# Last block's transposes and router products moved ahead of two panels and its second norm; deferred rows finished by VectorE in the second tile

## The reference

```python
shift1, scale1, gate1, shift2, scale2, gate2 = split(silu(cond) @ w_mod + b_mod, 6)
x = x + gate1 * rmsnorm(token_mixer(rmsnorm(x) * (1 + scale1) + shift1))
h = rmsnorm(x, g_pre2) * (1 + scale2) + shift2
x = x + gate2 * rmsnorm(hier_moe(h), g_post2)
# hier_moe: router products h @ w_rg (4 groups), h @ w_re (16 experts);
# best group, then the best 2 experts in it; for a chosen expert e:
#   a = silu(t @ w_eg[e]) * (t @ w_eu[e]);  y += gate[e] * (a @ w_ed[e])
```

## Time and profile before

| what | value |
|---|---|
| median of 3 runs | 684.89 us (684.49 to 685.68) |
| profiled execution, its own time | 689.32 us |
| its span | 687.6 us |
| PE busy | 656.3 us, 95% |
| DVE busy | 520.5 us, 76% |
| ACT busy | 416.5 us, 61% |
| POOL busy | 102.3 us, 15% |
| PE's share of the chain that ended last | 83% |
| mean rate of all transfers | 274 GB/s |

### The profile page before, as it was taken

One profiled execution on the slowest core, in us unless ns is written; L12 is line 12 of the kernel. 1 busy time (PEld: TensorE's weight loads), 2 busy tenths in 40 slices (PEclk: granted clock), 3 DMA queues, 4 the chain that ended last, 5 costly groups with the idle time before them and its releaser, 6 DMA issues.

```text
span 687.6 us, 10864 instructions
## 1 busy us (share of the span) xinstructions
PE 656.3 (95%) x3492; PEld 526.9 (77%) x3492; DVE 520.5 (76%) x756; ACT 416.5 (61%) x629; POOL 102.3 (15%) x150
## 2 busy tenths in 40 slices
PE   3999999999999999999989899999999999999983
PEld 0577767789999987778838688888888888888861
DVE  2667798656446468766579899999999999999966
ACT  5552222244434559884444578888888888888953
POOL 2030001055000000000013200000000000370361
PEclk9999999999999999999989999999999999999997
DMA  9975876539321243006798999999999999999586
GB/s 327 354 257 190 285 240 190 166 101 378 94 80 60 93 153 118 6 1 211 280 337 305 345 367 412 411 412 412 412 412 411 412 411 412 412 412 411 225 278 153
DMA packets 79002, 188.15 MB, mean 274 GB/s; under 512 B 7619, under 2 KB 29176, under 8 KB 78964
## 3 DMA queue, kind: packets, MB, share of 16 engines
q1 hardware_dynamic: 67456, 153.11, 60.3%
q0 software_dynamic: 7200, 22.47, 9.8%
q10 hardware_dynamic: 4310, 12.10, 4.4%
HBM read 166.12 MB, written 21.53 MB: 273 GB/s over the span
## 4 chain that ended last, share of the span: by engine, by line
PE 83%; DVE 6%; DMA 4%; SPq 2%; POOL 2%; issue 1%; ACT 1%; ACTq 0%; POOLq 0%; DVEq 0%
PE ps L2018 22%; PE ps L2038 11%; PE ps L1783 10%; PE ps L1843 8%; PE ps L1811 8%; PE ps L1815 5%; PE ps L1886 3%; PE ps L1716 3%; PE ps L1861 2%; PE ps L2001 2%; PE ps L1877 2%; SPq L403 2%; PE ps L1941 1%; DMA qkv_mem<-in_w_mod 1%; DMA catT_mem<-token_rows,token_lists 1%
## 5 line engine op out<-in xcount | busy, mean ns | idle before, releaser
L2018 PE MATMUL ps<-split_ring,split_rows 128*128 128x512 f32 x756 | 176.1, 392 | 1.2 <-DVE split_rows L1483 1.0
L2018 PEld LDWEIGHTS ps<-split_ring,split_rows 128*128 128x128 f32 x756 | 140.7, 188 | 30.5 <-DVE split_rows L1483 1.2
L1388 DVE TENSOR_TENSOR split_ring<-qkv_mem,split_ring 128x1024 fp32r<-128x1024 f32 x126 | 146.2, 1220 | 21.9 <-ACT split_ring L871 21.9
L871 ACT CAST split_ring<-qkv_mem 128x1024 fp32r<-128x1024 f32 x126 | 123.5, 1056 | 13.0 <-ACT catT_mem L995 9.2
L2038 PE MATMUL ps<-split_ring,split_rows 128*128 128x512 f32 x360 | 86.0, 394 | 0.0
L1811 PE MATMUL ps<-split_rows,split_ring 128*128 128x384 f32 x288 | 85.7, 345 | 0.2
L1815 PE MATMUL ps<-split_rows,split_ring 128*128 128x256 f32 x288 | 77.0, 280 | 0.0
L2038 PEld LDWEIGHTS ps<-split_ring,split_rows 128*128 128x128 f32 x360 | 66.5, 188 | 13.3
L1388 DVE TENSOR_TENSOR split_ring<-raw_ring,split_ring 128x1024 fp32r<-128x1024 f32 x64 | 74.2, 1221 | 0.0
L1783 PE MATMUL ps<-split_ring,split_rows 128*128 128x512 f32 x288 | 68.2, 393 | 0.0
L871 ACT CAST split_ring<-raw_ring 128x1024 fp32r<-128x1024 f32 x64 | 62.5, 1049 | 1.7 <-DMA raw_ring<-in_w_exp_up 1.7
(11 more groups left out here) (350 smaller groups left out, 928.0 us busy)
## 6 DMA issues: line engine op xcount, KB each, us to landing
qkv_mem<-in_w_exp_gate SPq DMA_DIRECT2D x64, 512.0 KB, 9.5
qkv_mem<-in_w_exp_up SPq DMA_DIRECT2D x60, 512.0 KB, 7.9
raw_ring<-in_w_exp_down SPq DMA_DIRECT2D x60, 512.0 KB, 9.5
raw_ring<-in_w_mod SPq DMA_DIRECT2D x28, 512.0 KB, 4.8
qkv_mem<-in_w_mod SPq DMA_DIRECT2D x32, 256.0 KB, 7.8
expert_rows<-catT_mem ACTq DMA_DIRECT2D x14, 512.0 KB, 6.7
expert_rows<-work POOLq DMA_DIRECT2D x26, 256.0 KB, 6.7
raw_ring<-in_w_in SPq DMA_DIRECT2D x12, 512.0 KB, 8.1
```

The costliest lines, as they stand in the source:

```text
L871: nc.scalar.copy(moe_split(tile, j, r, 0), moe_raw(tile, j, r)).then_inc(S["hi"], 1)
L1388: tt(moe_split(tile, j, r, 1), moe_raw(tile, j, r), moe_split(tile, j, r, 0).bitcast(F32), ALU.subtract).then_inc(S["lo"], 1)
L2018: ins = mm(ps[:, j, :], xS[:, s, k, :], moe_split(tile, j, k // 2, m)[:, (k % 2) * N:(k % 2 + 1) * N], start=(k == 0 and s + m == 0), stop ...
```

## The change

On PE, `row_transposes(4)`, `logits(3)` and `logits(4)` follow `late_panel(10, 0)` directly; `late_panel(11, 1)` comes after them. On DVE the last block's `second_norm` is cut in two: its reciprocal stays, its scale and shift move behind the ranking (`oh_ready`); the low part of the first gate panel's last quarter moves from there to behind `first_oh`. ACT issues the last block's rows for the gathers later (`h2_rows_out(4)`). POOL's four row operations leave POOL and become four DVE operations in the second tile, ahead of the early slots; POOL only issues the writes, behind its first two gathers. SP loads tile 1's gate panel before the first tile's up quarters, the up quarters 1 and 3 before 0 and 2, and `gate2` after all experts' weights.

```diff
 # SP
             late_half(10, 1)
+            expert_quarters((None, 1), 0, w_eg, slice(1, 2), (2, 3))
+            sp.wait_ge(S["mod_q"], MODQ + 6)
+            expert_quarters((None, 1), 0, w_eg, slice(1, 2), (0, 1))
+            sp.wait_ge(S["mod_q"], MODQ + 8)
+            expert_quarters((None, 0), 1, w_eu_first, slice(0, 1), (1, 3))
             sp.wait_ge(S["h2s"], TB)
             expert_quarters((None, 0), 1, w_eu_first, slice(0, 1), (0, 2))
-            sp.wait_ge(S["mod_q"], MODQ + 8)
-            expert_quarters((None, 0), 1, w_eu_first, slice(0, 1), (1, 3))
-            expert_quarters((None, 1), 0, w_eg, slice(1, 2))
             expert_quarters((None, 1), 1, w_eu, slice(1, 2))
-            sp.wait_ge(S["g_mm"], 2)
-            sp.wait_ge(S["modout0"], MODOUT + 16)
-            sp.wait_ge(S["modout1"], MODOUT + 16)
-            for c in range(2):
-                row_in(gate2, 5, c, S["gate_in"])
             expert_quarters((None, 1), 2, w_ed, slice(0, 1))
...
             expert_quarters((later, 2), 0, w_ed, expert_of((later, 1)))
+            sp.wait_ge(S["g_mm"], 2)
+            sp.wait_ge(S["modout0"], MODOUT + 16)
+            sp.wait_ge(S["modout1"], MODOUT + 16)
+            for c in range(2):
+                row_in(gate2, 5, c, S["gate_in"])
 # POOL
-            for n, c in enumerate(LATE):
-                pool.wait_ge(S["row_copied"], n + 1)
-                pool.wait_ge(S[f"modst{c % 2}"], MODST[c - 2] + 32)
-                pool.tensor_tensor(late_row(c), late_row(c), late_bias(c), ALU.add).then_inc(S["pool_chain"], 1)
-                pool.wait_ge(S["pool_chain"], n + 3)
-                pool.tensor_tensor(late_row(c), late_row(c), late_norm(c), ALU.mult).then_inc(S["mod_row"], 1)
-                pool.wait_ge(S["mod_row"], MOD_LATE - MOD_EARLY + n + 1)
-                pool.dma_start(mod_d[:, c * N:(c + 1) * N], late_row(c)).then_inc(S[f"modout{c % 2}"], 16)
...
+            for n, c in enumerate(LATE):
+                pool.wait_ge(S["mod_row"], MOD_LATE - MOD_EARLY + n + 1)
+                pool.dma_start(mod_d[:, c * N:(c + 1) * N], late_row(c)).then_inc(S[f"modout{c % 2}"], 16)
             with pool.Fori(0, last) as i:
 # ACT
             late_panel_out(1)
-            h2_rows_out(4)
...
             nc.scalar.activation(rw["e2"], rw["d2"], ACT.Exp).then_inc(S["exp0"], 1)
+            h2_rows_out(4)
 # DVE
             split_lo_moe((None, 0), 0, (2,))
-            second_norm(4)
-
+            dve.wait_ge(S["rt3s"], TB)
+            link(nc.vector.reciprocal(rs3[:, last_block:last_block + 1], rt3[:, last_block:last_block + 1]))
...
             tt(rw["d2"], rw["m2"], rw["m1"], ALU.subtract).then_inc(S["oh_ready"], 1)
 
-            split_lo_moe((None, 0), 0, (3,))
+            dve.wait_ge(S["norm2_in"], 64)
+            link(stt(h2[:, last_block, :], x[:, last_block, :], rs3[:, last_block:last_block + 1], scale2[:, 0, :], ALU.mult, ALU.mult))
+            tt(h2[:, last_block, :], h2[:, last_block, :], shift2[:, 0, :], ALU.add).then_inc(S["h2s"], 1)
             dve.wait_ge(S["cum_mm"], 1)
...
             ins.then_inc(S["first_oh"], 1)
+            split_lo_moe((None, 0), 0, (3,))
             dve.wait_ge(S["exp0"], len(UNITS) + 2)
...
             split_lo_moe((None, 1), 0, (3,))
+            for n, c in enumerate(LATE):
+                dve.wait_ge(S["row_copied"], n + 1)
+                dve.wait_ge(S[f"modst{c % 2}"], MODST[c - 2] + 32)
+                link(tt(late_row(c), late_row(c), late_bias(c), ALU.add))
+                tt(late_row(c), late_row(c), late_norm(c), ALU.mult).then_inc(S["mod_row"], 1)
 # PE
             late_panel(10, 0)
+            row_transposes(4)
             logits(3)
-            row_transposes(4)
+            logits(4)
+
             late_panel(11, 1)
-            logits(4)
-
             late_panel(10, 1)
```

More of the change, by code:

```diff
@@ L641, in _ @@
             pool.tensor_tensor(col(180), epsc, epsc, ALU.add).then_inc(S["pool_chain"], 1)
-            pool.wait_ge(S["pool_chain"], 3 + len(LATE))
+            pool.wait_ge(S["pool_chain"], 3)
             for b in range(TB):
```

## The result

The changed kernel takes 691.93 us (690.7 to 693.64, 4 runs) beside 685.28 (684.49 to 685.78, 4 runs) of the kernel before: ratio 1.0100, 95% interval 1.0074 to 1.0126. It is slower by 6.6 us where 2.05 us were forecast, and lies above the range. A second series gave 691.73 (690.62 to 698.0, 6 runs) beside 686.19: 1.0097 (1.0064 to 1.0130). Over 98 runs of the kernel before that went beside the experiments the median is 686.23, so the 684.89 on which the forecast stands was itself low by 1.3; against the wider base the loss is 5.5 to 5.7 us. Executions that took over 1.5% more than the fastest of their kernel are left out of every median here: one of the kernel before, two of e6 and one of e7.

What follows compares the result with a forecast made beforehand. PE, busy 95% of the span, was taken as the bound. Tile 1's gate product +0.1 us plus a PE stall of 1.95 gave +2.05: 684.89 to 686.9 us, 0.3% slower; range from 0.2 below 683.8 to 688.7.

Steps and rivals of the forecast that it cites:

- Part 1: PE's router products come earlier: logits(4) ends and DVE's ranking begins 1.98 us earlier.
- Part 2: DVE after the ranking: the moved norm, 2.46 us, spends the gain; L1450 starts about 0.1 us later.
- Part 3: POOL's row operations off DVE's list chain: four long steps shorten by 3.04 us together.
- Part 4: Later up quarters hold ACT, and with it DVE: quarter 0 lands at 363.3, `xT_lo` starts 1.35 us later.
- G: Start of tile 1's gate product on PE; forecast to move by +0.1 us (-1.2 to +1.4).
- Part 5: Four row operations on DVE, 2.7 us in all, stall PE once for 1.95 us within tile 1's 48 products.
- Part 6: Small parts: the later gather of tile 3, `gate2` at the end and later token rows each cost nothing.
- (a): Rival: up quarters in time, quarter 0 by 360.2, lists gain all 3.04; -1.1 us, 683.8; chance 0.17.
- (b): Rival: tile 1's gather lands sooner without `gate2` ahead, 2.9 us at most; -0.85 us, 684.0; chance 0.10.
- (c): Rival: PE's clock falls to half for a stretch after waits, 1.6 us more; +3.65 us, 688.5; chance 0.13.

Runs made afterwards that it cites:

- e6: Kernel before with the four row operations on DVE in the slack behind tile 1 and in tile 2, gate2 at the end: 685.34 us (0.9955 to 1.0009).
- e7: Changed kernel with 18 more idle-filling products on PE while it waits for the late rows' sums: 690.66 us (1.0041 to 1.0087).
- e8: Kernel before with PE's order alone changed: last transposes, both router products, then the two half panels: 686.81 us (0.9990 to 1.0025).
- e10: Kernel before with gate2 alone moved behind the last expert weights: 686.81 us (0.9989 to 1.0037).
- e11: Kernel before with SP's order alone changed: tile 1's gate panel ahead of the up panel, up quarters 1 and 3 before 0 and 2: 692.76 us.
- e17: Changed kernel with the norm back ahead of the ranking and SP's old order of the panels: 685.86 us (0.9976 to 1.0022).
- e3: Kernel before with the deferred rows moved to DVE at the changed kernel's place, gate2 at the end: 689.92 us (1.0022 to 1.0070).
- e9: e8 plus the row operations on DVE in the slack, POOL's writes behind its gathers, gate2 at the end: 684.07 us (0.9951 to 1.0000).
- e16: Changed kernel with the last block's norm back ahead of DVE's ranking, all else as changed: 691.81 us (1.0047 to 1.0093).
- e2: Changed kernel with the deferred rows' four operations back on POOL at their old place: 696.28 us (1.0089 to 1.0158).

## Why the prediction was wrong, step by step

**Part 1** was right in kind, and a third of its gain did not come: L1409 starts 1.29 us earlier, not 1.98. The 16 products of logits(4) take 2.77 us for 1.96, as the granted clock falls in the midst of them: it is 0.96 from 348.50 to 349.50 and 0.50 from 349.50 on. The forecast took their duration over.

**Part 2** was right as a sum: L1450 comes 0.68 later where 0.1 later was forecast, and Part 1's shortfall of 0.69 covers the difference. But it priced the moved norm on DVE alone, where "the 1.98 us gained is spent". e8 shows that with the norm left in place the gain lives in the trace: ranking waits for the products, the norm fits ahead of it.

**Part 3** was right: L1470, L1473, L1512 and L1514 take 0.24, 0.17, 0.17 and 0.43. The Trainium skill, "SBUF — State Buffer", section "SBUF: two separate sides", tells of this pair of engines that one blocks the other whole. The trace agrees: before, the long L1470 ended at 365.02, 0.11 us after POOL's operation. So does e8, where POOL still makes the rows and L1514 takes 1.38.

**Part 4 is the step that failed**, as a term too small: "The rest, 5.0 MB, takes 12.3 us: 363.3". The quarter was there at 368.07 on a trace that is 1.18 late, so 3.6 us later, beyond the bound of 364.6. The stretches tell why. (i) The forecast said that "the queue does not run dry in between". From 353 to 357 it moved 224 GB/s, not 408, since two of SP's gate quarters wait for the slow logits(4) and two for the panel 11 half behind it, and its up quarters, behind the last panel 10 half, are issued from 356.60 on: 4 x (408 - 224) = 0.74 MB, 1.8 us. (ii) By 368 it had moved 2.33 + 0.32 + 0.90 + 4.48 = 8.0 MB, not 7.34: 1.7 us. What got ahead of the quarter in those 0.7 MB no row tells. The nearest candidates are up quarter 2, issued at 359.5, half a us behind quarter 0, and landed at 369.3, and tile 1's up panel, issued from 360.0 on. The token rows, issued at 359.08 beside quarter 0, landed at 365.8, ahead of it, as the count had them. ACT's way from the quarter to `xT_lo` took 5.42 us, as forecast (5.3). So `xT_lo` moves by 5.04 in place of 1.35, and the end of L1514 by 3.76. G moved by 1.96, where the forecast had +0.1, and not by 3.76: the gather was no longer the last thing, as the earlier trace rows has it; PE's own 36 products and the transposes, from 380.86 to 390.2, were.

**Part 5** was right to 0.07 us: a stall of 1.88 for 1.95, once, with four operations of 0.68. What it left out is the clock behind it, 1.7 us in the first trace, none in the second.

**Part 6** was right about `gate2`: in e10 its place alone leaves the time unchanged (0.9989 to 1.0037). The waits of tile 3's gather and of the token rows have no run of their own; from tile 2 to the tail the traces of before and after take the same 230.3 us.

**The rivals.** (a), up quarters in time, fell with U. It looked for the cause in the moved norm; SP's order alone holds the quarters until 25.1 (e11), and with that order undone beside the norm, as in e17, the quarters are in time and the time is that of before. The forecast treated SP's order as a count of bytes on a full queue, and never asked what it alone would do to the kernel before. (b) came about by its sign, a gather under 7 us: from issue to landing it takes 5.8 us in the first trace of after, for 7.83. But it takes 5.7 in the second trace of before too, with `gate2` in its old place: the 7.83 was that of one execution, and `gate2` had no part in it. It brought no gain, since PE's own work ended later. (c), the clock, came about, on top of the late quarters: in after's first trace it is 0.8 in logits(4), 2.46 in the gate products and 1.7 behind the stall. The middle one lies inside the wait for the lists in part. The stretch at 0.54 that the forecast quotes for it would have allowed a term in the sum.

The sum as measured, on the first traces: G +1.96, stall +1.88, clock behind it +1.7, and 0.2 of smaller steps give D +5.7. The second traces give +4.3. The rest of the 5.5 to 6.6 us is not placed.

## What to carry to other kernels

When a transfer that an engine waits for in program order is put behind two others, try that edit alone in thought: its landing, then the first engine that waits for it, then all that stands behind that wait. Two edits that make the same transfer late hide one another, so undoing one of them proves nothing; undo both, or make each alone on the kernel before. A gain can hide as well: 3.0 us off DVE's lists was worth 0.3 to 0.9 in one order of PE's products and 3.0 in the other. And where PE waits for 2 us or more, as here, put a bound for slow products behind the wait into the sum.

## What was unexpected in the hardware

**The tail goes with the length of a tiny operation.** POOL's one-element operation ahead of the last gathers takes 3.58 us in the first trace of before, and 0.97 in the second, and the tail is 51.1 and 47.4 us. e3, e9 and e16, with tails of 51.0 or more, have it at 3.3 to 3.6 too; all ten traces with a tail under 49 have it at 1.3 or less. Three others, at 49.5 to 50.0 with a short operation, show that it is not all. DVE's four splits lie over it in both traces of before, 1.14 us apart: in the first it ends with the last of them (649.21, the splits 649.17), in the second with the one under which it began (647.31, and 646.04 + 1.22 = 647.26). Where it begins doesn't decide: in e9 and e2 alike it begins 0.02 us ahead of a split and takes 3.56 and 1.30. What does is open.

```profile
645.63 3.58 POOL L641 TENSOR_TENSOR small<-small 128x1 f32<-128x1 f32 x1 [31.23 <-DMA expert_rows<-catT_mem]
644.54 4.63 DVE L1388 TENSOR_TENSOR split_ring<-raw_ring,split_ring 128x1024 fp32r<-128x1024 f32 x4
```
```profile
646.34 0.97 POOL L641 TENSOR_TENSOR small<-small 128x1 f32<-128x1 f32 x1 [31.58 <-DMA expert_rows<-catT_mem]
644.90 4.63 DVE L1388 TENSOR_TENSOR split_ring<-raw_ring,split_ring 128x1024 fp32r<-128x1024 f32 x4
```

The operation's own 2.6 us are not the whole 3.7 of the tail. A kernel that is 3 or 5 us faster up to tile 2 could by this show 0 or 2 in its median; that this is why e9 does is not shown, as only one execution of it has a trace, and e8's has the short tail.

**The clock in one program is not the same in each execution**: the 24 products behind the same stall took 7.38 and 5.76 us in the two traces of the changed kernel. In two kernels that differ from it only ahead of the stall they took 5.78 (e7) and 7.35 (e16).
